# A two-layer decoder trunk on one core: the shared on-chip region starts at a multiple of 128 bytes instead of 32

## The reference

```python
def reference(x, positions, norm_gain, ffn_w_gate, ...):
    for layer in range(DEPTH):          # DEPTH = 2, D_MODEL = 1024, D_FF = 2816, SEQ = 512
        x = x + 0.5 * swiglu(rmsnorm(x, ...), w_gate, w_up, w_down)
        h = rmsnorm(x, norm_gain[layer, 1])
        if layer % 2 == 0:
            x = x + conv_sparse_attn_mixer(h, ...)   # short gated convolution || top-128 sparse attention
        else:
            x = x + gated_deltanet_mixer(h, ...)     # gated delta rule in chunks
        x = x + 0.5 * swiglu(rmsnorm(x, ...), w_gate, w_up, w_down)
    return rmsnorm(x, final_gain)

def swiglu(h, w_gate, w_up, w_down):
    return (jax.nn.silu(h @ w_gate) * (h @ w_up)) @ w_down
```

## The kernel before

| tensor | moving operand of L396 to L398 in | address before | modulo 128 |
|---|---|---|---|
| x | none | 16512 | 0 |
| h_hi, h_lo | gate, up and input projections | 32896, 49280 | 0, 0 |
| raw | none | 65664 | 0 |
| w_hi, w_lo | none (stationary) | 88192, 99456 | 0, 0 |
| consts | none | 110720 | 0 |
| silu_g, act_f, sq, sq_acc, rstd, hf | none | 118208 to 138688 | 64 |
| region0 | | 138688 | 64 |
| a_hi, a_lo | down projections | 138688, 183744 | 64, 64 |
| emix_hi, emix_lo | attention's out projection | 138688, 155072 | 64, 64 |
| omix_hi, omix_lo | delta rule's out projection | 138688, 155072 | 64, 64 |
| ev tensors from iq to probsT | none | 171456 to 228800 | 64 |
| od tensors from qc to e_last | none | 171456 to 210400 | 64 |
| v_beta, k_beg, k_dec, state, v_new | none | 210400 to 224736 | 96 |

## Time and profile before

### The profile page before, as it was taken

One profiled execution on the slowest core, in us unless ns is written; L12 is line 12 of the kernel. 1 busy time (PEld: TensorE's weight loads), 2 busy tenths in 40 slices (PEclk: granted clock), 3 DMA queues, 4 the chain that ended last, 5 costly groups with the idle time before them and its releaser, 6 DMA issues.

```text
span 2252.4 us, 26792 instructions
## 1 busy us (share of the span) xinstructions
PE 2203.3 (98%) x10238; PEld 1770.2 (79%) x10238; DVE 1121.4 (50%) x1596; ACT 859.0 (38%) x1102; POOL 243.3 (11%) x163
## 2 busy tenths in 40 slices
PE   7999999999999999999999999899999999999998
PEld 6888887666677888888888888678888877888886
DVE  4444444687644444423444432486676544444423
ACT  4333323224544333322333322557667554333221
POOL 1000000122211000000000000033333201000001
PEclk9999999999999999999999999999999999999999
DMA  5333322212113333332333332211111123333321
GB/s 168 96 93 102 113 91 71 73 57 66 47 57 94 94 102 93 111 100 79 93 93 97 113 103 80 67 38 38 38 38 38 38 76 93 98 98 93 118 94 50
DMA packets 49759, 185.89 MB, mean 83 GB/s; under 512 B 6544, under 2 KB 6544, under 8 KB 49680
## 3 DMA queue, kind: packets, MB, share of 16 engines
q1 hardware_dynamic: 49392, 184.77, 26.8%
q10 hardware_dynamic: 288, 0.03, 0.0%
HBM read 182.68 MB, written 2.10 MB: 82 GB/s over the span
## 4 chain that ended last, share of the span: by engine, by line
PE 91%; DVE 5%; ACT 2%; issue 1%; POOL 0%; DMA 0%; SPq 0%; DVEq 0%; ACTq 0%; POOLq 0%
PE prod L396 27%; PE prod L398 26%; PE prod L397 26%; PE misc L598 4%; PE misc L529 1%; PE prod L486 1%; PE misc L547 1%; DVE qc L1338 1%; PE misc L649 1%; ACT w_hi L736 1%; PE misc L621 1%; DVE w_lo L972 1%; DVE qc L1336 0%; PE misc L509 0%; PE misc L538 0%
## 5 line engine op out<-in xcount | busy, mean ns | idle before, releaser
L972 DVE TENSOR_TENSOR w_lo<-raw,w_hi 128x1024 fp32r<-128x1024 f32 (+1 forms) x300 | 404.8, 1349 | 762.2 <-ACT w_hi L736 761.4
L396 PE MATMUL prod<-h_hi,w_hi 128*128 128x512 f32 x1856 | 764.7, 412 | 0.6 <-DVE w_lo L972 0.3
L398 PE MATMUL prod<-h_hi,w_lo 128*128 128x512 f32 x1856 | 725.8, 391 | 0.0
L397 PE MATMUL prod<-h_lo,w_hi 128*128 128x512 f32 x1856 | 724.8, 391 | 0.0
L736 ACT ACTIVATE w_hi<-raw 128x1024 fp32r<-128x1024 f32 (+1 forms) x317 | 356.0, 1123 | 598.5 <-PE prod L398 586.9
L396 PEld LDWEIGHTS prod<-h_hi,w_hi 128*128 128x128 f32 x1856 | 350.2, 189 | 104.5 <-issue 38.5
L397 PEld LDWEIGHTS prod<-h_lo,w_hi 128*128 128x128 f32 x1856 | 350.2, 189 | 73.5 <-issue 10.6
L398 PEld LDWEIGHTS prod<-h_hi,w_lo 128*128 128x128 f32 x1856 | 349.2, 188 | 74.7
L396 PE MATMUL prod<-a_hi,w_hi 128*128 128x512 f32 x704 | 277.4, 394 | 0.0
L398 PE MATMUL prod<-a_hi,w_lo 128*128 128x512 f32 x704 | 276.0, 392 | 0.0
L397 PE MATMUL prod<-a_lo,w_hi 128*128 128x512 f32 x704 | 273.2, 388 | 0.0
(11 more groups left out here) (226 smaller groups left out, 2070.2 us busy)
## 6 DMA issues: line engine op xcount, KB each, us to landing
raw<-in_w SPq DMA_DIRECT2D x253, 512.0 KB, 3.6
raw<-in_wd SPq DMA_DIRECT2D x64, 704.0 KB, 4.1
x<-in_x SPq DMA_DIRECT2D x8, 256.0 KB, 6.2
out<-y_out SPq DMA_DIRECT2D x8, 256.0 KB, 2.2
consts<-in_consts SPq DMA_DIRECT2D x1, 896.0 KB, 8.6
raw<-in_w SPq DMA_DIRECT2D x2, 256.0 KB, 4.5
hf<-in_pos SPq DMA_DIRECT2D x1, 256.0 KB, 9.7
od_conv<-in_od_conv SPq DMA_DIRECT2D x1, 48.0 KB, 2.2
```

Of the source, the lines that this page charges most:

```text
L396: pe.matmul(bank, wh, hi, start=first and k == 0, stop=False)
L397: pe.matmul(bank, wh, lo, start=False, stop=False)
L398: ins = pe.matmul(bank, wl, hi, start=False, stop=last and k == tiles_n - 1)
L972: dve.tensor_tensor(w_lo[:, n % 2, 0:w], raw[:, n % 4, 0:w], w_hi[:, n % 2, 0:w].bitcast(F32), ALU.subtract).then_inc(lo_ready, 1)
```

## The change

The start of the shared region is rounded up to a multiple of 128 instead of 32 bytes. It becomes 138752 instead of 138688, and all tensors of the three sets, with the three placed relative to `region0` (`o_n`, `q_dec`, `neg_w`), move up by 64 bytes. Within a set the distances stay as they are, since `Plan` still rounds to 32. Nothing else is different: the same instructions in the same order with the same waits.

```diff
         region = nc.sbuf_base
-        region0 = (region + 31) // 32 * 32
+        region0 = (region + 127) // 128 * 128
         region_end = nc.sbuf_usable_end
```

## The result

The changed kernel is slower: 2262.57 us (median of 6 runs, 2261.57 to 2265.07) against 2250.05 us of the kernel before (6 runs, 2247.33 to 2254.2). The ratio is 1.0053, 95% interval 1.0041 to 1.0065, or 9.2 to 14.6 us. The forecast was 2246.3 us, 0.26% faster, with a range up to 2254.5.

What follows compares the result with a forecast made beforehand. PE, busy 98% of 2252.4 us, was taken to bound the kernel through the distance between large-matmul starts. 832 k-steps gain 5.8 us, other parts 0: 2254.17 - 5.8 = 2248.4, or 2246.3 us on the median's scale; range 2242.5 to 2254.5.

Steps and rivals of the forecast that it cites:

- What bounds the kernel: Whole kernel: PE busy 98% of 2252.4 us, so time is the number of large matmuls times the distance between starts.
- The two paces, 679.9 and 686.9, and that they come from the place of the moving tile: Large products: a k-step takes 679.9 ns out of h, 686.9 out of a; the moving operand's place makes the difference.
- 832 k-steps of them, all on the path: Down and out projections: 704 k-steps from a, 64 each from emix and omix, all setting the end; 5.8 us gained.
- Its offset modulo 128 is the plainest difference of place: Moving tiles of the region: starting at 64 modulo 128 makes their k-steps 7 ns slower than h's, at 0.
- the term of the sum, -7.0 ns for each of 832 k-steps: Down and out projections: each k-step falls from 686.9 to 679.9 ns, together 5.8 us faster.
- Rival 2: K-steps out of the region: moving stream and weight load clash by their distance, making it slower; 2258.8 us, chance 0.06.
- Rival 1: Large products: height or a coarser pairing with weight tiles matters, not modulo 128; 64 bytes move nothing, 2252.1 us, chance 0.26.
- Small matmuls, VectorE, ScalarE, transfers at 0: Other users of the region: each taken as 0; bounds 1.8 us for small matmuls, 2.3 for VectorE and ScalarE, either way.
- The clue that was misread: L396 to L398: uneven modelled durations out of a were tied to its unaligned place; 389 ns in all three expected afterwards.
- The two rules weighed in the prediction: Large matmuls: about 216 ns set by 512 columns alone, and SBUF lines of 16 bytes; by either the gain is 0.

Runs made afterwards that it cites:

- at distance 0: Shared region 192 bytes higher than in the kernel before, its moving tiles 0 modulo 512 from the weight tiles: 2247.55 us against 2253.03, ratio 0.9975.
- The map: Separate kernel of 128x512 products alone, moving and weight tiles placed at varied offsets: 226.7 to 234.2 ns per product on the 32-byte grid.

## Why the prediction was wrong, step by step

- *What bounds the kernel* was right: the time moved with the distance between the starts of large matmuls, and all other engines and the waits stayed within 0.4 us, or 0.5 for a wait.
- *The two paces, 679.9 and 686.9, and that they come from the place of the moving tile*: right, and on record before the run. *832 k-steps of them, all on the path*: right, 832 x 13.1 ns gives 10.9 us against the measured 9.2 to 14.6, and at distance 0, 832 x 6.9 gives 5.7 us, a ratio of 0.9975, which is what was measured there.
- *"Its offset modulo 128 is the plainest difference of place"*: this is the step that failed. Two paces at two places fit any rule in which the places differ. The table of addresses also held that h is at a multiple of 512 from the weights and a at 64 modulo 256; the runs show that this is the difference that counts, and the change made it 128, one of the bad values. So the term of the sum, -7.0 ns for each of 832 k-steps, had the wrong sign: it measured +13.1. The map gives five of the eight distances on the 32-byte grid within 0.1 ns of 233.4, one at 234.2, and only 0 and 64 below: the region happened to lie at the second best of eight, and on that grid a move to any place but distance 0 had to lose. Nobody could read this from the trace of before. But with two paces known and the new distance seen in no row, a slower one deserved more than 6%.
- *Rival 2* (a clash with the weight loads, by distance) named what counts, the distance, and the sign, with a chance of 0.06. Its price was too small: 8 ns over the present step, put together from one uneven duration, where 13.1 were measured; 2258.8 us instead of 2262.57. The range stopped below it.
- *Rival 1* (height, or a coarser pairing with the weight tiles) named the pairing too, but assumed that 64 bytes would move nothing in it; a period of 256 is one in which 64 bytes do.
- *Small matmuls, VectorE, ScalarE, transfers at 0*: right. L598 and L612 still have a median of 275 ns, and PEld, DVE, ACT and POOL are busy within 0.4 us of before.
- *The clue that was misread*: 394, 388 and 392 ns for the three products out of a was taken as a mark of "unaligned" (the 392 is L398: `L398 PE MATMUL prod<-a_hi,w_lo x154: 392/392/392, 2129.6 to 2234.7; 128*128 128x512 f32 x154`). In the map the same spread belongs to distance 64 (388/392/398), and 389/389/389 to distance 0. The change did not make the durations even: L396 has 392/398/398.

The two rules weighed in the prediction would both have given no change, so neither accounts for what was measured. (The 216 ns of the first are that section's figure for an isolated product.) A third one bears on the cause. The Trainium skill, "TensorE: Matmul & The Clock Gate" (section "Step-by-step: what each phase is for"), says: "Loading the next tile's weights doesn't steal SBUF read bandwidth from the running matmul." Here the pace of the same product goes from 226.7 to 240 ns with the distance of the two tiles alone, and moving only w_lo costs 13.5 ns a step; for rounded float32 at 512 columns the runs speak against it, in plain float32 they show nothing against it.

## What to carry to other kernels

Where PE is busy without a break, take the distance between starts of the same product from different tiles out of the trace; a difference of 1 to 3% at the same clock can come from where the moving tile and the weight tile lie relative to each other. For 128x512 rounded float32, put both at the same place modulo 256 (measured best, 680 against up to 703 ns per three products on a 32-byte grid) and do it on purpose, since every small tensor allocated in between shifts it. With 256 columns another distance was the best of four, so try it out for your shape. Aligning one of the tiles to a rounder number does not do it; two paces in one trace tell that place matters, and not by which rule.

## What the runs showed of the hardware that was not expected

- The distance of moving and weight tile sets the pace of a 128x512 product in rounded float32 between 226.7 and 240 ns, with nothing else running, and on a 32-byte grid the pattern repeats with 256 bytes. Distance 112 is as good as 0; 20 and 36 are the worst of those tried.
- With 256 columns the order changes (120.0 ns at 0, 113.4 at 192), with 128 columns and in plain float32 next to nothing is to be seen (111.3 to 111.7 ns, and 429 ns a record) at the distances tried.
- A pair of tiles at a bad distance can lengthen two products, the one that uses the weights and the one before it. Whether the 226.7 ns themselves still hold a clash of the two streams was not settled.
- In the attention layer's input projections, with small matmuls between the k-steps, a bad distance cost 6 ns a k-step instead of 20.1.
